# Norms over 1024 features: sums and roots with tokens on partitions, spread again by TensorE

## What is computed

```python
def rms_norm(x, g):
    xf = x.astype(jnp.float32)
    y = xf * lax.rsqrt(jnp.mean(xf * xf, axis=-1, keepdims=True) + EPS)
    return (y * g.astype(jnp.float32)).astype(x.dtype)

def modulate(x, g, shift, scale):
    return rms_norm(x, g) * (1 + scale) + shift
```

## Time and profile before

| | before |
|---|---|
| median of 3 runs | 4107.0 us (4097.72 to 4107.02) |
| the profiled execution | 4103.4 us, its span 4101.6 us |
| PE busy | 3832.3 us, 93% |
| DVE, ACT, POOL busy | 46%, 36%, 39% |
| mean granted TensorE clock | 0.973 of full |
| DMA | 101 GB/s over the span |

### The profile page before, as it was taken

The page is one execution under the profiler, slowest core; times in us unless marked ns, Lnnn a source line. Parts: engine busy times, 40 slices in busy tenths (PEclk is TensorE's granted clock), DMA queues, the critical chain, the costliest instruction groups (busy, mean ns, idle before and its releaser), DMA issues. The chain is left out here.

```text
span 4101.6 us, 52392 instructions
## 1 busy us (share of the span) xinstructions
PE 3832.3 (93%) x19218; PEld 3034.3 (74%) x19218; DVE 1886.7 (46%) x3264; ACT 1480.8 (36%) x2293; POOL 1614.1 (39%) x801
## 2 busy tenths in 40 slices
PE   6987899999898889999999889999999999899999
PEld 5876688888666668887888753788878877547887
DVE  2775766543646566655554845222232232452222
ACT  3264532222336563333222554322232233533222
POOL 1320243444330046654455321455555553115554
PEclk9999999999999999999999998999999999989999
DMA  7610134442110027663665310233323332102332
GB/s 248 193 37 24 52 117 139 144 128 64 39 47 1 19 75 230 225 200 109 226 219 169 84 47 1 67 97 93 97 83 97 97 90 65 42 1 82 97 98 77
DMA packets 460503, 411.96 MB, mean 100 GB/s; under 512 B 28096, under 2 KB 405312, under 8 KB 460352
## 3 DMA queue, kind: packets, MB, share of 16 engines
q1 hardware_dynamic: 457903, 408.65, 32.2%
q10 hardware_dynamic: 2448, 1.32, 0.1%
HBM read 406.25 MB, written 7.60 MB: 101 GB/s over the span
## 5 line engine op out<-in xcount | busy, mean ns | idle before, releaser
L220 POOL TENSOR_TENSOR s_wlo<-s_raw,s_whi 128x1024 fp32r<-128x1024 f32 x490 | 1179.9, 2416 | 1941.3 <-ACT s_whi L212 1940.9
L234 PE MATMUL psum<-s_xhi,s_whi 128*128 128x512 f32 x3264 | 1226.3, 376 | 18.2 <-POOL s_wlo L220 8.6
L235 PE MATMUL psum<-s_xlo,s_whi 128*128 128x512 f32 x3264 | 1219.6, 374 | 0.0
L236 PE MATMUL psum<-s_xhi,s_wlo 128*128 128x512 f32 x3264 | 1216.4, 373 | 0.0
L212 ACT ACTIVATE s_whi<-s_raw 128x1024 fp32r<-128x1024 f32 x490 | 510.2, 1056 | 1660.1 <-PE psum L236 1656.0
L234 PEld LDWEIGHTS psum<-s_xhi,s_whi 128*128 128x128 f32 x3264 | 615.4, 189 | 135.5 <-issue 11.5
L235 PEld LDWEIGHTS psum<-s_xlo,s_whi 128*128 128x128 f32 x3264 | 615.3, 189 | 111.1 <-issue 3.3
L236 PEld LDWEIGHTS psum<-s_xhi,s_wlo 128*128 128x128 f32 x3264 | 614.4, 188 | 111.9
L234 PE MATMUL psum<-s_ahi,s_whi 128*128 128x512 f32 x1232 | 468.9, 381 | 11.6 <-DVE s_y L1300 7.2
L236 PE MATMUL psum<-s_ahi,s_wlo 128*128 128x512 f32 x1232 | 465.4, 378 | 0.0
L235 PE MATMUL psum<-s_alo,s_whi 128*128 128x512 f32 x1232 | 462.6, 375 | 0.0
(11 more groups left out here) (306 smaller groups left out, 4274.5 us busy)
## 6 DMA issues: line engine op xcount, KB each, us to landing
...
```

Source lines behind the costliest of these rows:

```text
L220: pool.tensor_tensor(K.wlo[:, c % HL, 0:a * b], K.raw[:, c % RAW, 0:a * b], K.whi[:, c % HL, 0:a * b].bitcast(F32), ALU.subtract).then_inc ...
L234: pe.matmul(out, lh, rh, start=first, stop=False)
L235: pe.matmul(out, lh, rl, start=False, stop=False)
L236: return pe.matmul(out, ll, rh, start=False, stop=last)
```

## The change

The sums and the roots of the nine norms are turned around. `columns` takes a tile of squares, 128 features by 128 tokens, as the stationary operand and moves one column of `s_mean_d` through it: the result is one column with tokens on the partitions, T / 128 columns per tile of squares. Each partial sum gets columns of its own in PSUM. DVE adds them with one `tensor_reduce` (`newton`), ACT's guess (`guess`) and the three Newton steps work on T / 128 columns instead of T, and `repeat` has PE spread the result over all partitions again: the column, repeated as stationary operand, times the identity, 128 x 128 for each 128 tokens, into the PSUM tile `factor()` that the DVE products read.

POOL adds only the first 7 squares behind a projection, and the first 5 (wide) or 4 (narrow) behind a feed-forward; the other squares go to PE directly, and POOL's sum goes last but one. In `InnerNorm` the 25 or 32 `hold` matmuls become 4 between sums and `repeat`, 14 behind it, and 3 or 4 behind the columns of each tile of `h`. `PreNorm` gets 4. `warm` runs 4 and 7 (wide) or 3 and 5 (narrow); the lot that waited for the guess is gone. New semaphores: `y_seen`, `sq_seen`, `col_total`, `root_ready`, `factor_ready`.

```diff
--- before.py
+++ after.py
...
@@ -145,12 +145,10 @@
         K = self.K
-        wide = T == T0
         chunk_ops(K, pe, c)
-        for n, name, value in ((8 if wide else 6, None, 0), (14 if wide else 11, "r0_ready", 0),
-                               (7 if wide else 5, "xm_full", -7)):
+        for n, name in ((4 if T == T0 else 3, None), (7 if T == T0 else 5, "xm_full")):
             if name:
-                pe.wait_ge(self.sem[name], self.at(name, value))
+                pe.wait_ge(self.sem[name], self.at(name, -7))
             for _ in range(n):
                 pe.matmul(self.slot(T, 0, BANK), K.whi[:, c % HL, 0:P], K.whi[:, c % HL, 0:BANK], start=True, stop=True)
@@ -644,14 +642,60 @@
         self.low(e)
-class Squares:
-    def begin(self, kind):
-        self.kind, self.added, self.done, self.split_after = kind, 0, 0, []
+class Columns:
+    def columns(self, e, total, x, i):
+        w = self.T // P
+        for j in range(w):
+            ins = e.matmul(total[:, i * w + j:i * w + j + 1], x[:, j * P:j * P + P], self.K.mean_d[:, 0:1], start=True, stop=True)
+        return ins
+    def col(self, i):
+        return self.K.rcol[:, i, 0:self.T // P]
+    def guess(self, e, n):
+        e.wait_ge(self.sem["col_total"], self.at("col_total", n + 1))
+        e.activation(self.col(0), self.col(2), ACT.Abs_reciprocal_sqrt, bias=self.K.eps[:, 0:1]).then_inc(self.sem["r0_ready"], 1)
+    def newton(self, e, total, parts, n):
+        K, w = self.K, self.T // P
+        r, tmp, x = (self.col(i) for i in range(3))
+        e.tensor_reduce(out=x, in_=total[:, 0:parts * w].rearrange("p (i j) -> p j i", i=parts), axis=AX_X,
+                        op=ALU.add).then_inc(self.sem["col_total"], 1)
+        e.wait_ge(self.sem["r0_ready"], self.at("r0_ready", n + 1))
+        e.scalar_tensor_tensor(out=tmp, in0=x, scalar=EPS, in1=r, op0=ALU.add, op1=ALU.mult).then_inc(K.sem["dve_step"], 1)
+        e.wait_ge(K.sem["dve_step"], K.step())
+        e.scalar_tensor_tensor(out=tmp, in0=tmp, scalar=-0.5, in1=r, op0=ALU.mult, op1=ALU.mult).then_inc(K.sem["dve_step"], 1)
+        e.wait_ge(K.sem["dve_step"], K.step())
+        e.scalar_tensor_tensor(out=r, in0=tmp, scalar=1.5, in1=r, op0=ALU.add, op1=ALU.mult).then_inc(self.sem["root_ready"], 1)
+        e.wait_ge(self.sem["factor_ready"], self.at("factor_ready", n + 1))
+    def repeat(self, e, n):
+        K = self.K
+        e.wait_ge(self.sem["root_ready"], self.at("root_ready", n + 1))
+        for j in range(self.T // P):
+            ins = e.matmul(self.factor()[:, j * P:j * P + P], self.col(0)[:, j:j + 1].to_broadcast([P, P]), K.ident[:, :],
+                           start=True, stop=True)
+        ins.then_inc(self.sem["factor_ready"], 1)
+class Squares(Columns):
+    def begin(self, kind, pool_adds):
+        self.kind, self.added, self.done, self.split_after, self.pool_adds = kind, 0, 0, [], pool_adds
     def square(self, k):
         n, T = (2, self.T) if self.T == T0 else (3, self.T)
@@ -667,12 +711,12 @@
         self.done = k + 1
         self.tile_done(e, k)
         if k >= n:
-            used = self.kind + "_used"
-            e.wait_ge(self.sem[used], self.at(used, k - n + 1))
+            name, past = (self.kind + "_used", 0) if k - n < self.pool_adds else (self.kind + "_seen", self.pool_adds)
+            e.wait_ge(self.sem[name], self.at(name, k - n + 1 - past))
         e.activation(self.square(k), self.tile(k), ACT.Square).then_inc(self.sem[self.kind + "_sq"], 1)
     def add(self, e, k):
-        if k < 0:
+        if k < 0 or k >= self.pool_adds:
             return
         self.added = k + 1
         acc, used = self.K.rstd[:, 0:self.T], self.kind + "_used"
@@ -684,7 +728,7 @@
             e.tensor_tensor(acc, acc, self.square(k), ALU.add).then_inc(self.sem[used], 1)
     def pool(self, e):
-        for k in range(self.added, 8):
+        for k in range(self.added, self.pool_adds):
             self.add(e, k)
         for c in self.split_after:
             split_lo(self.K, e, c)
@@ -693,20 +737,26 @@
         e.wait_ge(self.sem["ada_read"], self.ada_read)
         e.wait_ge(self.sem["bias_ready"], self.at("bias_ready"))
-        e.wait_ge(self.sem[self.kind + "_used"], self.at(self.kind + "_used", 8))
-        for a, w in parts(self.T):
-            ins = e.matmul(self.total()[:, a:a + w], self.K.mean_d[:, :], self.K.rstd[:, a:a + w], start=True, stop=True)
-        ins.then_inc(self.sem[self.kind + "_total"], 1)
+        for k in range(self.pool_adds, 8):
+            if k == 7:
+                e.wait_ge(self.sem[self.kind + "_used"], self.at(self.kind + "_used", self.pool_adds))
+                self.columns(e, self.total(), self.K.rstd, 0)
+            e.wait_ge(self.sem[self.kind + "_sq"], self.at(self.kind + "_sq", k + 1))
+            self.columns(e, self.total(), self.square(k), k + 1 - self.pool_adds).then_inc(self.sem[self.kind + "_seen"], 1)
+    def sum_up(self, e):
+        parts = 9 - self.pool_adds
+        e.wait_ge(self.sem[self.kind + "_seen"], self.at(self.kind + "_seen", parts - 1))
+        self.newton(e, self.total(), parts, 0)
     def first_root(self, e):
-        K, T = self.K, self.T
         for k in range(self.done, 8):
             self.squared(e, k)
-        e.wait_ge(self.sem[self.kind + "_total"], self.at(self.kind + "_total", 1))
-        e.activation(K.rstd[:, 0:T], self.total(), ACT.Abs_reciprocal_sqrt, bias=K.eps[:, 0:1]).then_inc(self.sem["r0_ready"], 1)
+        self.guess(e, 0)
         for c in self.split_after:
-            split_hi(K, e, c)
+            split_hi(self.K, e, c)
 class InnerNorm(Squares, Norm):
@@ -715,14 +765,15 @@
     def __init__(self, K, T, post, pre, out):
+        self.begin("y", 7 if isinstance(out, Proj) else 5 if T == T0 else 4)
         super().__init__(K, T, post, pre)
         self.act_lo, self.ada_read, self.tile_done, out.norm = self.at("act_lo"), K.ada_tasks, self.y_read, self
-        self.begin("y")
     def counts(self):
         c = super().counts()
         c.update(self.ring_counts(self.T, 1))
-        c.update(sq_ready=8, sq_used=7, y_sq=8, y_used=8, y_total=1)
+        m = self.pool_adds
+        c.update(sq_ready=8, sq_used=7, y_sq=8, y_used=m, y_seen=8 - m, col_total=2, root_ready=2, factor_ready=2)
         return c
     def total(self):
@@ -745,40 +796,29 @@
     def pe(self, e):
         K, T = self.K, self.T
+        wide = T == T0
         self.summed(e)
-        self.hold(e, 25 if T == T0 else 32, 1 if T == T0 else 5)
+        self.hold(e, 4, 1 if wide else 5)
+        self.repeat(e, 0)
+        self.hold(e, 14, 1 if wide else 5)
         self.take(e, T, 0)
         for k in range(8):
             e.wait_ge(self.sem["sq_ready"], self.at("sq_ready", k + 1))
-            for a, w in parts(T):
-                ins = e.matmul(self.slot(T, 0)[:, a:a + w], K.mean_d[:, :], K.t1[:, k % 2, a:a + w],
-                               start=(k == 0), stop=(k == 7))
-            ins.then_inc(self.sem["sq_used" if k < 7 else "out_ready"], 1)
+            self.columns(e, self.slot(T, 0), K.t1[:, k % 2, :], k).then_inc(
+                self.sem["sq_used" if k < 7 else "out_ready"], 1)
+            self.hold(e, 4 if wide and k < 7 else 3, 1 if wide else 5)
+        self.repeat(e, 1)
     def act(self, e):
         K, T = self.K, self.T
         self.first_root(e)
-        self.squares(e, 0, K.h, self.h_there)
+        for k in range(8):
+            self.h_there(e, k)
+            if k >= 2:
+                e.wait_ge(self.sem["sq_used"], self.at("sq_used", k - 1))
+            e.activation(K.t1[:, k % 2, 0:T], K.h[:, k, 0:T], ACT.Square).then_inc(self.sem["sq_ready"], 1)
+        self.guess(e, 1)
         self.high(e)
-    def rstd_free(self, act):
-        act.wait_ge(self.sem["h_ready"], self.at("h_ready", 8))
-    def root(self, e, n, total):
-        K = self.K
-        e.wait_ge(self.sem["r0_ready"], self.at("r0_ready", n + 1))
-        r, tmp = K.rstd[:, 0:self.T], self.total()
-        e.scalar_tensor_tensor(out=tmp, in0=total, scalar=EPS, in1=r, op0=ALU.add, op1=ALU.mult).then_inc(
-            self.free(self.T, 0) if n else K.sem["dve_step"], 1)
-        if n:
-            e.wait_ge(self.free(self.T, 0), self.is_read(self.T, 0))
-        else:
-            e.wait_ge(K.sem["dve_step"], K.step())
-        e.scalar_tensor_tensor(out=tmp, in0=tmp, scalar=-0.5, in1=r, op0=ALU.mult, op1=ALU.mult).then_inc(K.sem["dve_step"], 1)
-        e.wait_ge(K.sem["dve_step"], K.step())
-        e.scalar_tensor_tensor(out=tmp, in0=tmp, scalar=1.5, in1=r, op0=ALU.add, op1=ALU.mult).then_inc(K.sem["dve_step"], 1)
-        e.wait_ge(K.sem["dve_step"], K.step())
     def dve(self, e):
         K, T = self.K, self.T
@@ -787,18 +827,19 @@
             e.tensor_tensor(K.coef[:, 16 * s:16 * s + 8], K.mod[:, gate:gate + 8], K.cols[:, g:g + 8], ALU.mult).then_inc(K.sem["dve_step"], 1)
             e.wait_ge(K.sem["dve_step"], K.step())
             self.gains(e, s)
-        self.root(e, 0, self.total())
```

(29 more changed lines are left out.)

2 lines of the change are left out of this document (1 added, 1 removed).

## The result

The changed kernel takes 4121.9 us at the median of seven runs (4112.4 to 4123.5), the kernel before 4106.2 (4097.7 to 4109.6). The ratio is 1.0033, 95% interval 1.0024 to 1.0042: slower, where 4063 was forecast and 4043 to 4083 was the range. The profiled execution took 4112.4, its span 4110.5 against 4101.6. It is the fastest of the seven.

A forecast was written before the change was run, and what follows sets the result against it. TensorE, busy for 93% of the span, was taken as the bound. Savings of 32.0 + 3.2 + 11.2 - 5 = 41.4 from 4103.4 gave 4062, put at 4063 us for the median; range 4043 to 4083.

The forecast's parts named there:

- the term for the clock: Thinner PE work may keep 1.2 GHz into the first real matmuls at nine places and some holds: 5 us lost.
- the price of a column sum: One-column sum on PE: 0.08 us per record, 0.16 per 128-token tile, 0.26 cold; record range 0.031 to 0.11.
- first roots, to first use of the factor: Nine norms, to first use of the first factor: fewer GpSimd adds, roots on 4 to 6 columns; 32.0 us saved.
- second roots, first to second factor: Four InnerNorms, root taken after the h tiles: 1.5 us saved in each wide one, 0.1 narrow, 3.2 together.
- Rival C: Clock stays at 1.2 GHz through h stages and 5.6 us into each next product: slower, 4116 us; chance 0.05.
- rival A: Each column-sum record costs 0.11 us (0.16 cold), making PE the bound in h stages: 4078 us; chance 0.20.
- First roots behind a feed-forward: GpSimd adds only four or five squares, PE sums the others: 4.5 us saved in each narrow norm, 5.2 wide.
- First roots behind a projection: GpSimd drops only its last add: 3.1 us saved in each PreNorm, 1.2 in each InnerNorm.
- The chain from last sum to first use: From the last column sum to the first use of the factor: 2.75 us narrow, 3.2 wide.
- Filler lag: Filler before the next product cut, so its first real matmul lags its operand less: 11.2 us over seven narrow norms.
- this comes through: In narrow stages PE, at 1.36 us a tile, is slower than VectorE, so the 11.2 us shortens the kernel.
- the reduction: VectorE's adding of partial column sums, at most 40 values a partition: taken as 0.2 us (0 to 0.7).

The follow-up runs named there:

- the first three experiments: Changed kernel with wide second roots as before the change (4090.4), or with no fillers (4097.9) or seven fillers (4102.3) per tile in the wide h stages.

## Why the prediction was wrong

The forecast was 46.4 saved and 5 lost to the clock. Its failing step is that 5: the term for the clock left out the wide h stages. They took 24.0 us longer than before, and 22.9 of that came with the fall of the clock, since with 128 columns and the same fillers they take 23.6 each. Second comes the price of a column sum. The parts as forecast, and as the two first profiles have them (positive is saved):

| | forecast | measured |
|---|---|---|
| first roots, to first use of the factor | 32.0 | 12.8 |
| second roots, first to second factor | 3.2 | -27.1 |
| from there to the first real matmul | 11.2 | 13.3 |
| clock | -5 | in the rows above and below |
| outside the norms | 0 | -8.0 |
| sum | 41.4 | -8.9 |

- **The clock in the h stages.** The working let it cost "half the rate for about 1 us in each of nine places and some of the holds". Measured, by the granted clock: about 30 of 37 us of one wide stage and 22 of 33 of the other at 1.2 GHz, and the stages 14.0 and 9.9 longer than before. Rival C had this mechanism, priced at 9.7 for a wide stage, and I gave it 0.05. My argument against it, that dense fillers stand before the real matmuls, was about the next products and not about the stage itself. C was wrong in two points: narrow stages kept the clock with three fillers a tile, and the feed-forwards behind the norms started warm (361.6 in all). Its time of 4116 came near by luck: these two losses of 15 and 25 weren't there, but neither was most of the 32.0 that it, too, took as saved in the first roots (12.8), and 8.0 were lost outside the norms.
- **The price of a column sum.** I took 0.08 for a record. It measured 0.11 at full clock, the upper bound, and 0.21 at half, above the bound of 0.16. By this rival A was right on the price: a narrow tile 1.60 (its 1.57), a wide one 2.27 (its 2.24), PE slower than VectorE in both. With the clock held and nothing else changed (128 columns, all fillers) the kernel took 4080; A said 4078.
- **First roots behind a feed-forward.** Forecast 4.5 saved to first use in each narrow one, 5.2 wide. Measured 2.1 to 2.8 and 0.5: 20 sums of tiles at 0.22 instead of 0.16, and repeats at half clock. With 128 moving columns 3.6, with one tile fewer on PE 4.4, wide 4.6.
- **First roots behind a projection.** PreNorms 3.1 forecast, 2.7 and 0.8 measured, by whether the clock held; InnerNorms 1.2 forecast, 0.4 (narrow) and 0.7 (wide) lost, 0.9 and 0.6 gained with 128 columns.
- **Second roots.** 1.5 wide and 0.1 narrow forecast. With the clock held and the fillers gone it was 1.0 and 0.5 to 0.6. The chain from last sum to first use was right: 2.6 at 2968 to 2972, forecast 2.75.
- **Filler lag.** 11.2 forecast over seven norms. In these seven 9.5 of it went: 0.15 is left in five and 0.5 in two. The wide norms, counted at nothing, gave 3.8 more. But the cut alone, put into the kernel before, bought 7.6 in the norms, and 4.5 of that was given back in the products behind them. Ahead of mixers a wait for GpSimd took a part of its place. The sentence "this comes through" looked at the first few tiles of the product, not at what PE meets 18 us later.
- **Right were** the reduction (0.18, taken as 0.2), the Newton steps (0.16, taken as 0.21) and the order of who waits for whom up to the first real matmul. The nine norms with 128 columns and no fillers sum to 181.8, 41.5 below 223.3. That this is nearly the 41.4 of the forecast is luck: 24.4 in the first roots instead of 32.0, 3.1 in the second, 14.0 instead of 11.2 behind them, and none of the 5 lost.
- **The arithmetic.** The median of 4107.0 less 41.4 gives 4065.6, not 4063: only 1 of the 3.6 between profile and median was added, and less for the rivals. It changes no reading.

What is open: the mixers' stretches at the low clock, and why they fall differently from run to run; and 7 to 10 us by which the first three experiments beat the expectation, of which the later profiles put a part in the mixers, and a part in that the changed kernel's fastest run was the basis of all my sums.
